# Seven-product FFN blocks on one Trainium2 core: a weight sum moved from a DMA to VectorE, two form operations one product later, and one sum on GpSimd

## The reference

```python
def swiglu(h, w_gate, w_up, w_down):
    return (jax.nn.silu(h @ w_gate) * (h @ w_up)) @ w_down

x = x + 0.5 * swiglu(rmsnorm(x, norm_ffn1[layer]), ffn1_gate[layer], ffn1_up[layer],
                     ffn1_down[layer])
```

## Time and profile before

| | before |
|---|---|
| median of three runs | 3648.75 us (3647.11 to 3653.2) |
| profiled execution | 3649.27 us |
| its span | 3647.4 us |
| busy: TensorE, VectorE, ScalarE, GpSimd | 97%, 69%, 49%, 8% |
| granted TensorE clock, mean | 0.994 |
| matmuls at L670 on split weights | 2955.3 us, x16236 |
| GpSimd transfers ring<-arena (24 of 1 MB, 4 of 0.5 MB) | 28 |
| GpSimd transfers ring<-ring (28 of 1 MB, 4 of 0.5 MB) | 32 |

### The profile page before, as it was taken

How to read it: one execution, slowest core, us unless ns; L and a number is a source line. 1 busy time by engine, 2 the same in 40 slices (tenths; PEclk the granted TensorE clock), 3 DMA queues, 4 the chain that set the end, 5 groups by cost and what they waited for, 6 DMA issues and landing times.

```text
span 3647.4 us, 53611 instructions
## 1 busy us (share of the span) xinstructions
PE 3543.2 (97%) x20848; PEld 3028.1 (83%) x20848; DVE 2513.1 (69%) x3210; ACT 1804.8 (49%) x2527; POOL 285.7 (8%) x317
## 2 busy tenths in 40 slices
PE   9999899999999999999999999999999999999999
PEld 7776688888678887989977798999998977789988
DVE  4455666666755767787767577887888676578885
ACT  3335344436633444655555456555655554546554
POOL 0001000000200000100000220000000000310000
PEclk9999999999999999999999999999999999999999
DMA  4000256422005663577621016776777421017774
GB/s 185 36 35 35 92 162 183 140 105 93 24 35 173 173 174 117 172 199 221 176 87 57 12 53 172 201 217 179 204 204 194 133 106 50 2 63 210 207 197 132
DMA packets 70668, 475.18 MB, mean 130 GB/s; under 512 B 7952, under 2 KB 8336, under 8 KB 17552
## 3 DMA queue, kind: packets, MB, share of 16 engines
q1 hardware_dynamic: 46224, 303.97, 23.0%
q0 software_dynamic: 24192, 167.78, 21.0%
HBM read 404.62 MB, written 2.10 MB: 112 GB/s over the span
## 4 chain that ended last, share of the span: by engine, by line
PE 75%; DVE 16%; ACT 5%; DMA 2%; issue 2%; DVEq 0%; POOL 0%; ACTq 0%; SPq 0%; POOLq 0%
PE ps L670 73%; DVE split L2531 6%; ACT arena L1479 3%; DVE arena L2531 3%; PE ps L679 2%; DVE X L2535 2%; ACT split L1479 2%; DMA ring<-in_wts 2%; DVE arena L2535 2%; ACT L1479 1%; DVE arena L3629 0%; DVE ring L2531 0%; DVE small L2547 0%; DVE arena L2527 0%; DVE arena L2559 0%
## 5 line engine op out<-in xcount | busy, mean ns | idle before, releaser
L670 PE MATMUL ps<-split 128*128 128x512 f32 (+1 forms) x16236 | 2955.3, 341 | 51.2 <-DVE arena L2531 14.1
L670 PEld LDWEIGHTS ps<-split 128*128 128x128 f32 x16236 | 2506.9, 191 | 419.3 <-issue 60.3
L2531 DVE TENSOR_TENSOR split<-ring,split 128x1024 fp32r<-128x1024 f32 x674 | 823.0, 1221 | 422.7 <-ACT split L1479 372.6
L1479 ACT ACTIVATE split<-ring 128x1024 fp32r<-128x1024 f32 x674 | 709.7, 1053 | 720.9 <-PE ps L670 660.4
L1479 ACT ACTIVATE arena<-ps 128x512 f32<-128x512 f32 (+5 forms) x656 | 343.0, 523 | 377.1 <-PE ps L670 258.3
L670 PE MATMUL ps<-arena 128*128 128x128 f32 (+9 forms) x3344 | 485.5, 297 | 23.2 <-ACT arena L1479 8.8
L670 PEld LDWEIGHTS ps<-arena 128*128 128x128 f32 (+2 forms) x3344 | 393.8, 190 | 98.0 <-issue 65.6
L1479 ACT ACTIVATE split<-arena 128x1024 fp32r<-128x1024 f32 (+2 forms) x242 | 251.8, 1040 | 211.6 <-PE ps L670 131.4
L2531 DVE TENSOR_TENSOR split<-arena,split 128x1024 fp32r<-128x1024 f32 (+2 forms) x242 | 290.2, 1199 | 79.6 <-ACT split L1479 60.1
L2531 DVE TENSOR_TENSOR arena<-arena 128x512 f32<-128x512 f32 (+7 forms) x302 | 215.2, 713 | 32.7 <-ACT arena L1479 15.7
L2535 DVE SCALAR_TENSOR_TENSOR X<-ps,X 128x512 f32<-128x512 f32 x252 | 174.4, 692 | 69.0 <-PE ps L670 47.5
(11 more groups left out here) (114 smaller groups left out, 1214.2 us busy)
## 6 DMA issues: line engine op xcount, KB each, us to landing
ring<-in_wts SPq DMA_DIRECT2D x260, 1024.0 KB, 5.4
arena<-in_wts POOLq DMA_DIRECT2D x80, 1024.0 KB, 8.4
ring<-ring POOLq DMA_DIRECT2D x28, 1024.0 KB, 9.5
ring<-arena POOLq DMA_DIRECT2D x24, 1024.0 KB, 7.7
ring<-in_wts SPq DMA_DIRECT2D x41, 512.0 KB, 3.5
ring<-in_wts POOLq DMA_DIRECT2D x14, 1024.0 KB, 8.0
arena<-arena POOLq DMA_DIRECT2D x6, 1024.0 KB, 10.3
arena<-in_wts POOLq DMA_DIRECT2D x8, 512.0 KB, 4.5
```

Source lines behind the costliest of these rows:

```text
L670: return e.matmul(out, l, r, start=start, stop=stop, skip_group_check=True)
L1479: o.sig(a.activation(out, i, f, **kw), sig)
L2531: o.sig(v.tensor_tensor(out, a, b, op), sig)
```

## The change

- **T2 in gate blocks.** In the gate blocks 512 wide that aren't the first of their FFN (`B.adds`, four of each FFN), T2 is no longer a transfer. A new function `second(U, y)` on VectorE adds b12's slot (which holds T1) and b22's into b11's slot, one half behind each of the two splits of round 1, and signals `f_two`. T4's transfer, and the loads that take the slots of b12 and b22, wait for `f_two` there. Down blocks and the narrow block keep the transfer.
- **Down block D's first forms.** On VectorE, form(D.a11) and F7's sum go from round 1 to round 2. ScalarE's part of form(D.a11) stays in round 1.
- **Down blocks.** The second split of N5 goes ahead of form(f6) on VectorE. F3's sum, a12 = sum + a12, goes from VectorE to GpSimd, where it stands behind T2's transfer and ahead of T4's, waits for F6's sum, and signals `f_third`, for which ScalarE's form(f3) waits.
- **First blocks.** On ScalarE the reading of N5's result is put ahead of N3's second split, and the `extra` operations move by one place on both engines; on VectorE the form of f5 goes ahead of F6's sum, and F3's sum there is one step later.
- `f_open` is a new semaphore for the first block's opening transfer, which had `f_two` before.

```diff
--- before.py
+++ after.py
@@ -243,7 +243,7 @@
 def plan():
 
     lins, loads, turned, forms, n = {}, [], [], [], 0
-    sums, shapes, before, blocks, summed_up, done, holds = 0, 0, None, 0, 0, 0, {}
+    sums, shapes, before, blocks, summed_up, seconds, downs, thirds, done, holds = 0, 0, None, 0, 0, 0, 0, 0, 0, {}
     slots, held, kept = [0, 1, 2, 3], {}, {}
 
     def load(name, key, k0, nk, c0, ncol):
@@ -371,7 +371,7 @@
     mlp(1)
 
     def ffn(l, n_):
-        nonlocal n, blocks, summed_up, shapes, done
+        nonlocal n, blocks, summed_up, seconds, downs, shapes, thirds, done
         key, new, us = f"fgu{n_}_{l}", [], []
         old = [(len(turned) % 3, turned[-3] + 1), ((len(turned) + 1) % 3, turned[-2] + 1), ((len(turned) + 2) % 3, turned[-1] + 1)]
         if n_ == 2:
@@ -403,7 +403,7 @@
             return pc
 
         def block(name, key, p, h, kbase, c1, c2, w, at=None):
-            nonlocal blocks, summed_up
+            nonlocal blocks, summed_up, seconds, downs
             blocks += 1
             B = lins[name] = Block(name, h, p, w, at, 16 * blocks)
             B.begin, B.before = n, us[-1] if us else None
@@ -423,21 +423,31 @@
             for pc in B.of[2]:
                 summed_up += 1
                 pc.sum = ("f_t1", summed_up)
+            B.adds = B.gated and w == 512 and not B.first
+            downs += 16 * (not B.adds)
+            for pc in next(of for (what, _, _), of in zip(B.order, B.of) if what == "P6"):
+                seconds += B.adds
+                pc.sum = ("f_two", seconds) if B.adds else ("f_t2", downs)
+            B.two = pc.sum
             for q, b, added in (("b11", "t2", "f_t4"), ("b12", "t1", None), ("b22", "b22", None), ("b21", "t4", None)):
                 B.loads[q].end, B.loads[q].added = ("lo", end[b]), added and (added, B.count)
+            if B.adds:
+                B.loads["b12"].added = B.loads["b22"].added = B.two
             return B
 
         def down(B, a, b):
-            nonlocal shapes
+            nonlocal shapes, thirds
             end = {what: of[-1].i + 1 for (_, _, what), of in zip(ORDER, B.of)}
-            for what, buf, y in (("a11", 0, None), ("f7", 3, 1), ("a12", 1, None), ("f5", 2, 3), ("f6", 0, 2), ("f3", 1, 4), ("a22", 2, None)):
+            for what, buf, y in (("a11", 0, None), ("f7", 3, 1), ("a12", 1, None), ("f5", 2, 3), ("f6", 0, 2), ("f3", 1, None), ("a22", 2, None)):
                 f = Form(len(forms), what, 0, B.h, None, holds.get(buf))
                 f.end, f.gated, f.buf, f.sum = end[what], True, buf, y and shapes + y
                 holds[buf] = f.end
                 f.uses = {"a11": ("u", b.done), "a12": ("u", b.done + 2)}.get(what)
                 forms.append(f)
                 B.forms.append(f)
-            shapes += 4
+            shapes += 3
+            thirds += 1
+            B.forms[5].sum = ("f_third", thirds)
 
         row = held[slots[2]].key[0:2] in ("g1", "g2")
         if row:
@@ -1506,7 +1516,7 @@
         elif f.up:
             a.wait_ge(*emptied(f.up, 3))
         if f.sum:
-            a.wait_ge(S["shape"], f.sum)
+            a.wait_ge(*((S["f_third"], f.sum[1]) if isinstance(f.sum, tuple) else (S["shape"], f.sum)))
         act(next(K.m.formed(f)), K.m.source(f), ACT.Copy, "fhi")
 
     def formed(fs):
@@ -2155,10 +2165,8 @@
             if U.done:
                 a.wait_ge(S["u"], U.done)
             early(U, "P1", lambda t: F.part[:, 2 * t:2 * t + 2, :], 1.0)
-            next(extra)
             split(next(below))
             next(extra)
-            split(next(below))
 
         def gate_up(U, D):
 
@@ -2172,10 +2180,14 @@
                     if U.before and not U.before.gated:
                         a.wait_ge(S["form"], U.before.forms[6].i + 1)
                     early(U, "N5", lambda t: at(U, t, 1), 1.0)
+                    if U.first:
+                        split(next(below))
                 if U.order[r - 1][0] == "P6":
                     early(U, "P6", lambda t: at(U, t, 0), -1.0)
                 if wide and r == 5:
                     gated(U, 0, 0)
+                if U.first and r > 2:
+                    next(extra, None)
                 for y, _ in enumerate(() if U.first and r == 2 else U.of[r]):
                     split(next(below))
                     if wide and r == 5 and y == 0:
@@ -2755,6 +2767,14 @@
         for p in U.of[2][q:q + 1]:
             c = slice(p.q * U.w, (p.q + p.c) * U.w)
             tt(r["b12"][:, c], r["b12"][:, c], r["b11"][:, c], ALU.add, "f_t1")
+
+    def second(U, q):
+
+        r = {b: K.RING[:, ld.slot, :] for b, ld in U.loads.items()}
+        v.wait_ge(S[f"ring{U.loads['b22'].slot}"], U.loads["b22"].landed)
+        p = U.of[2][q]
+        c = slice(p.q * U.w, (p.q + p.c) * U.w)
+        tt(r["b11"][:, c], r["b12"][:, c], r["b22"][:, c], ALU.add, "f_two")
 
     def ln_join(name, key, splits):
 
@@ -3349,8 +3369,9 @@
                 for j in (0, 1):
                     v.wait_ge(*emptied(own_, j, g))
                 if g == 0:
+                    lo("f5", F.shape, 1)
                     tt(F.sixth, F.shape, F.a11, ALU.subtract, "h_sum")
-                    lo("f5", F.shape, 1)
+            yield
             tt(F.a12, F.sixth, F.a12, ALU.add, "h_sum")
             yield
             lo("f3", F.a12, 2)
@@ -3425,8 +3446,8 @@
             split(next(below))
             next(extra)
             split(next(below))
+            next(extra)
             split(next(below))
-            next(extra)
 
         def gate_up(U, D, late):
 
@@ -3458,6 +3481,8 @@
                     if r + y == 0 and not U.before.gated:
                         next(late)
                         next(late)
+                    if U.adds and not U.first and r == 1:
+                        second(U, y)
                     if D and r == 4:
                         added_up(after, y)
                     if r == 6 and y == 0:
@@ -3467,7 +3492,7 @@
                             added_up(after, 0)
                     if U.first:
                         next(extra, None)
-                if D and r == 1:
+                if D and r == 2:
                     form(D.forms[0])
                     tt(K.m.quarter(D.forms[1], "a21"), K.m.quarter(D.forms[1], "a11"), K.m.quarter(D.forms[1], "a21"), ALU.subtract, "shape")
                 if D and r == 3:
@@ -3490,9 +3515,8 @@
             form(f5)
             split(next(below))
             read(U, "P1")
+            split(next(below))
             form(f6)
-            split(next(below))
-            tt(q["a12"], q["sum"], q["a12"], ALU.add, "shape")
             split(next(below))
             split(next(below))
             form(f3)
@@ -3891,7 +3915,7 @@
         g.wait_ge(S["lo"], U.split["b11"])
         g.wait_ge(S["f_t1"], U.of[2][-1].sum[1])
         ld = U.loads["b11"]
-        g.dma_start(K.RING[:, ld.slot, 0:U.h * U.w], W["wts"][U.loads["b12"].i], accum_op=ALU.add).then_inc(S["f_two"], 16)
+        g.dma_start(K.RING[:, ld.slot, 0:U.h * U.w], W["wts"][U.loads["b12"].i], accum_op=ALU.add).then_inc(S["f_open"], 16)
 
     def block(U):
 
@@ -3899,23 +3923,24 @@
         b12, b22 = (W["wts"][U.loads[q].i] for q in ("b12", "b22"))
         t3 = (F.t3first if U.first else F.t3)[:, 0:n]
         if U.first:
-            g.wait_ge(S["f_two"], begun)
+            g.wait_ge(S["f_open"], begun)
             g.dma_start(at["b11"], b22, accum_op=ALU.add).then_inc(S["f_t2"], 16)
-            g.wait_ge(S["used"], U.begin)
-            g.dma_start(t3, b22).then_inc(S["f_base"], 16)
-            g.wait_ge(S["f_base"], U.count)
-            g.dma_start(t3, b12, accum_op=ALU.add).then_inc(S["f_t3"], 16)
-        else:
-            g.wait_ge(S["lo"], U.before.split["t3"])
-            g.dma_start(t3, b22).then_inc(S["f_base"], 16)
-            g.wait_ge(S["f_base"], U.count)
-            g.dma_start(t3, b12, accum_op=ALU.add).then_inc(S["f_t3"], 16)
+        g.wait_ge(*((S["used"], U.begin) if U.first else (S["lo"], U.before.split["t3"])))
+        g.dma_start(t3, b22).then_inc(S["f_base"], 16)
+        g.wait_ge(S["f_base"], U.count)
+        g.dma_start(t3, b12, accum_op=ALU.add).then_inc(S["f_t3"], 16)
+        if not U.adds and not U.first:
             g.wait_ge(S["lo"], U.split["b11"])
             g.wait_ge(S["f_t1"], U.of[2][-1].sum[1])
             g.wait_ge(S["f_t3"], U.count)
             g.dma_start(at["b11"], t3, accum_op=ALU.add).then_inc(S["f_t2"], 16)
+        if not U.gated:
+            f6, f3 = U.forms[4:6]
+            a12, total = K.m.quarter(f3, "a12"), K.m.quarter(f3, "sum")
+            g.wait_ge(S["shape"], f6.sum)
+            g.tensor_tensor(a12, total, a12, ALU.add).then_inc(S["f_third"], 1)
         g.wait_ge(S["lo"], U.split["b21"])
-        g.wait_ge(S["f_t2"], U.count)
+        g.wait_ge(S[U.two[0]], U.two[1])
         g.dma_start(at["b21"], at["b11"], accum_op=ALU.add).then_inc(S["f_t4"], 16)
 
     def unit(name, begun=None):
...
```

(2 more changed lines are left out.)

## The result

The changed kernel takes 3669.13 us (median of 6 runs, 3667.44 to 3673.36) against 3647.93 us of the kernel before beside it (6 runs, 3644.47 to 3654.88): ratio 1.0056, 95% interval 1.0044 to 1.0067, so 20 us slower. The forecast was 3649 us with a range of 3633 to 3662. It is outside.

What follows compares the result with a forecast made beforehand. TensorE, at 97% of the span, was taken as the bound, so only its stops could be won. Against 3649.3 us, -15.3 + 10 + 2.3 + 3 = 0.0 gave 3649 us, range 3633 to 3662.

Steps and rivals of the forecast that it cites:

- T2 on VectorE: Gate blocks: T4 starts earlier, b12 lands in time, N4's stops shrink to 0.25 us in all blocks: -15.3 us.
- gu101 2.8 + 2.5, gu113 ..., gu213 ...: Gate blocks ahead of down blocks: stops and lower-clock costs to be won, with gu103's 0.3 making up the -15.3 us.
- I take it as landed by 2296.5, with half a microsecond to spare: Gate blocks, in gu201's time: b12's load lands by 2296.5, before added_up needs it at 2296.9.
- Late b12: Rival: b11's later load and T4's transfer push b12 past its need in eight blocks: 3664 us, chance 0.13.
- The down blocks: Down blocks: GpSimd's addition holds VectorE, 0.8 us more a block, TensorE's stop moves to P2's first piece: +10 us.
- if the split is first, I wrote, the addition waits for it: Down blocks: GpSimd's addition and VectorE's split exclude each other, the later waits; the split behind then waits for the addition.
- Cheap sum: Rival: GpSimd's addition holds VectorE not at all or by some tenths; down blocks give -6: 3632 us, chance 0.30.
- (b): Down blocks: TensorE's stop of 0.84 us at the second piece of N5, in five of eight.
- The -6: Down blocks without exclusion: VectorE has 1.33 us less work, -1.2 us in each of five blocks.
- The first blocks: First block of each FFN: new order brings a stop at P6; gu110 loses 1.5 us, gu100 1: +2.3 us.
- end where they do now: First blocks gu200 and gu210: no loss, as their N3 ran at the lower clock and hid such a wait.
- Clock: TensorE's new stops bring two drops to the lower clock at 1.5 us each: +3 us.

Runs made afterwards that it cites:

- e0: Kernel before with only the change's two added semaphore names, unused: 3649.29 us, ratio 0.9999.
- e7: Kernel before with the down blocks' part alone (F3's sum on GpSimd, N5's split ahead of F6): 3661.37 us, ratio 1.0022.
- e12: Kernel before with N5's split ahead of F6 and F3's sum as a transfer that adds; T2 stays a transfer: 3644.91 us, ratio 0.9988.
- e8: Changed kernel with T4's transfer cut from 2048 to 128 columns ahead of down blocks (output not the reference's): 3657.51 us, one run.
- e3: Changed kernel with the two T2 additions each ahead of N5's split instead of behind it: 3658.47 us, ratio 1.0025.
- e1: Changed kernel with F3's sum back on VectorE behind form(F6), N5's second split still ahead of F6: 3662.51 us, ratio 1.0038.
- e10: Changed kernel with T2's additions ahead of N5's splits, first blocks as before, F3's sum as a transfer that adds: 3628.53 us, ratio 0.9938.
- e2: Changed kernel with the first block of each FFN in the order of before: 3660.03 us, ratio 1.0028.
- e11: Changed kernel with T2's additions ahead of N5's splits, first blocks as before, F3's GpSimd sum started behind N5's first split: 3639.01 us, ratio 0.9964.

## Why the prediction was wrong

**T2 on VectorE (forecast -15.3 us, measured 0).** Two things failed. First the size of the prize: "gu101 2.8 + 2.5, gu113 ..., gu213 ..." were the stops of one profiled execution. The same code in these eight blocks has an excess of 18.9, 9.5, 9.6 and 13.5 us in the four executions of it that were profiled (before, e0, e7, e12). With T2 as a transfer T4 starts anywhere from 10.4 to 18.8 us after the block's start, and each execution hits other blocks. Second, and this is the step that failed, "I take it as landed by 2296.5, with half a microsecond to spare": in that count b12 had to land 25.6 us after the start and landed at 26.7 to 27.9. I had taken b12 to be last and partly alone; but T4's transfer runs beside it nearly all its way and doubles it (e8). This was the rival *Late b12*, 1.1 to 2.3 us late, with 0.13. It names b11's later load beside T4's transfer; e8 leaves b11's load where it is, and b12 is in time. The rest of the working held: T4 did start at 13.4 in all eight, and the additions cost VectorE nothing that TensorE saw, for the gate blocks that aren't ahead of a down block have no stop with them. The gain was one place further up (e3).

**The down blocks (forecast +10, measured +8 within 4; in the traces +9 to +14).** The mechanism was right and a little undersized: the addition took 2.52 us in the mean, not 2.3, and held VectorE by 2.43, not 2.1. The detail was off: if the split is first, I wrote, the addition waits for it. In fd200 the split had begun 0.24 us ahead and was held all the same, by 2.80: that the later of the two waits doesn't show in that row. The stop moved to P2's first piece in seven blocks, as forecast. *Cheap sum* fell. One sentence failed that the +10 doesn't rest on: that with N5's split ahead of F6 "by this alone (b) is gone". With that order and the sum on VectorE the stop only moved to P6 (e1). The timeline had shown one late split, and I took the order of the work for its cause. The cause was the amount of it, as the windows over the whole stretch show; I had noted that VectorE has no gap there and didn't draw this from it. The -6 for one operation less was right: with nothing that holds VectorE the down blocks fell from 8.4 to 3.0 (e10).

**The first blocks (forecast +2.3, measured +6.5 in the traces, 9 in the times of e2).** The stop at P6 came in all four, about 2 us. The step that failed is that gu200 and gu210 "end where they do now", because their N3 ran at the lower clock and hid such a wait. In gu200 that clock was one execution's: in the other nine with the old order it has an excess of 5.3 to 5.8 us in place of 7.3, with the new order 7.6 in the mean. In gu210 it wasn't (7.2 to 7.7 in eight of the nine), and yet the new order costs 1.0 there in the mean. Together that is 3 us of the 6.5. gu100 and gu110 were undersized, 1.6 and 2.1 in place of 1 and 1.5.

**Clock (forecast +3).** In the FFNs the clock fell to 1.2 GHz in five places before and in three after. So the term had the wrong sign. In the 14 profiled executions it is one to five places; the excess above holds their cost.

**The sum.** By the traces: ahead of the down blocks +3 against the mean of the four executions (15.9 against 12.9), down blocks +10.5 to +13.6, first blocks about +6: 20 to 23, against 20 measured. The rest of the 24 us between the two profiled executions lies outside the FFNs, where their beginnings alone differ by 10. The failed 15.3 alone gives 3664 us, the figure of *Late b12*, outside the range; the undersized terms add the rest.

## What to carry to other kernels

Take the size of a prize from more than one execution when the stops hang on transfers: a program that differs only in names had half of them. Where an engine ends late, count its whole work over the stretch before reordering it; if it has no gap, only taking work away helps, and e10 shows that a queue that adds while it writes can take it. GpSimd gave back more than it took as long as its addition ran beside VectorE's SBUF operations. When a transfer must be early, ask what shares its way, and start that earlier instead of hoping for a margin of half a microsecond.

## What the runs showed of the hardware

GpSimd's addition of 128x1024 with both inputs in SBUF held a VectorE operation of the same kind for nearly as long as it ran: 2.43 us lost for 2.52 in the mean of eight, 2.80 for 2.69 where the split had begun 0.24 us ahead (fd200). In e3 and e8 an operation that had begun over 0.5 us ahead kept its 1.23 us, and the one behind it was held. VectorE's operations with an input in PSUM stayed as they were beside it, 1.49 us for two (e11). The Trainium skill says this of the two forms (SBUF — State Buffer, Who interferes with whom), and both halves agree with e11. A load of 1 MB took 4.7 to 5.0 us with little beside it (e8) and 9.5 to 10.8 beside an SBUF-to-SBUF transfer that adds and was issued 3.7 us ahead of it. In e0's gu111 that transfer was issued 0.9 us behind the load, and the load took 5.2. A transfer of 1 MB that adds within SBUF took 8.4 to 10.6 us (e10).
